# VectorE makes the fourth gate/up unit's low part before the sums of x in four feed-forward layers of a three-layer transformer kernel

## The reference

```python
def swiglu(x, w_gu, w_down):
    gate, up = jnp.split(x @ w_gu, 2, axis=-1)      # w_gu: 1024 x 5632
    return (jax.nn.silu(gate) * up) @ w_down        # w_down: 2816 x 1024

h = h + 0.5 * rmsnorm_2(swiglu(rmsnorm_2(h, g[0]), w_gu, w_down), g[1])
```

## Time and profile before

| what | value |
|---|---|
| time, median of 3 runs | 1271.47 us (1270.14 to 1271.62) |
| profiled execution, from first to last instruction | 1269.6 us |
| TensorE busy (matmul) | 1253.5 us, 99% |
| TensorE weight loads | 1028.9 us, 81% |
| VectorE | 1042.7 us, 82% |
| ScalarE | 804.0 us, 63% |
| GpSimd | 192.4 us, 15% |
| mean DMA rate | 218 GB/s |

### The profile page before, as it was taken

The page is one execution under the profiler, slowest core; times in us unless marked ns, Lnnn a source line. Parts: engine busy times, 40 slices in busy tenths (PEclk is TensorE's granted clock), DMA queues, the critical chain, the costliest instruction groups (busy, mean ns, idle before and its releaser), DMA issues.

```text
span 1269.6 us, 15538 instructions
## 1 busy us (share of the span) xinstructions
PE 1253.5 (99%) x5897; PEld 1028.9 (81%) x5897; DVE 1042.7 (82%) x1035; ACT 804.0 (63%) x986; POOL 192.4 (15%) x224
## 2 busy tenths in 40 slices
PE   9999999999999999999999999999999999999998
PEld 7888878888888878788778888788888877788886
DVE  6766689999799996767899997999977568999984
ACT  6674576665576664645766664766656466766662
POOL 6142130110001100102201101111001003301100
PEclk9999999999999999999999999999999999999999
DMA  9537498997649955568979978389745535999931
GB/s 333 174 100 231 133 313 254 268 270 248 201 151 255 269 168 180 188 226 215 320 249 245 271 251 255 116 237 274 219 166 173 184 125 168 315 286 262 266 135 44
DMA packets 143002, 277.32 MB, mean 218 GB/s; under 512 B 8992, under 2 KB 39896, under 8 KB 142928
## 3 DMA queue, kind: packets, MB, share of 16 engines
q1 hardware_dynamic: 120192, 229.67, 51.6%
q0 software_dynamic: 22288, 45.54, 19.7%
q10 hardware_dynamic: 448, 1.12, 0.2%
HBM read 275.24 MB, written 1.05 MB: 218 GB/s over the span
## 4 chain that ended last, share of the span: by engine, by line
PE 77%; DVE 12%; issue 4%; ACT 3%; DMA 3%; POOL 0%; DVEq 0%; SPq 0%; ACTq 0%
PE B L2102 14%; PE B L2104 14%; PE B L2103 14%; DVE w_lo L1359 7%; PE B L2558 6%; PE B L2560 6%; PE B L2559 6%; PE T L2102 3%; PE T L2104 3%; PE T L2103 3%; DMA VD<-in_ffn_w_gu 2%; DVE VD L1378 1%; DMA Z<-in_ffn_w_gu 1%; ACT w_hi L1082 1%; ACT w_hi L768 1%
## 5 line engine op out<-in xcount | busy, mean ns | idle before, releaser
L1359 DVE TENSOR_TENSOR w_lo<-w_raw,w_hi 128x2048 fp32r<-128x2048 f32 x129 | 296.5, 2299 | 87.5 <-ACT w_hi L768 87.2
L768 ACT ACTIVATE w_hi<-w_raw 128x2048 fp32r<-128x2048 f32 x129 | 247.1, 1918 | 102.7 <-PE B L2560 60.3
L2102 PE MATMUL B<-w_hi,xt_lo 128*128 128x512 f32 x652 | 260.5, 400 | 5.1 <-DVE w_lo L1359 2.1
L2104 PE MATMUL B<-w_hi,xt_hi 128*128 128x512 f32 x652 | 254.7, 391 | 0.0
L2103 PE MATMUL B<-w_lo,xt_hi 128*128 128x512 f32 x652 | 254.0, 390 | 0.0
L2558 PE MATMUL B<-w_hi,act_lo 128*128 128x512 f32 x440 | 172.5, 392 | 0.8 <-DVE w_lo L1359 0.4
L2560 PE MATMUL B<-w_hi,act_hi 128*128 128x512 f32 x440 | 171.4, 390 | 0.0
L2559 PE MATMUL B<-w_lo,act_hi 128*128 128x512 f32 x440 | 171.3, 389 | 0.0
L2102 PEld LDWEIGHTS B<-w_hi,xt_lo 128*128 128x128 f32 x652 | 122.4, 188 | 36.1 <-issue 6.2
L2104 PEld LDWEIGHTS B<-w_hi,xt_hi 128*128 128x128 f32 x652 | 122.4, 188 | 26.4
L2103 PEld LDWEIGHTS B<-w_lo,xt_hi 128*128 128x128 f32 x652 | 122.6, 188 | 23.3
(11 more groups left out here) (330 smaller groups left out, 2110.0 us busy)
## 6 DMA issues: line engine op xcount, KB each, us to landing
w_raw<-in_ffn_w_down SPq DMA_DIRECT2D x88, 512.0 KB, 5.8
Z<-in_ffn_w_gu SPq DMA_DIRECT2D x64, 512.0 KB, 8.1
w_raw<-in_ffn_w_gu SPq DMA_DIRECT2D x48, 512.0 KB, 5.2
nat<-in_ffn_w_gu SPq DMA_DIRECT2D x32, 512.0 KB, 7.8
QT<-in_ffn_w_gu SPq DMA_DIRECT2D x32, 512.0 KB, 7.0
Z<-in_ffn_w_gu POOLq DMA_DIRECT2D x32, 512.0 KB, 8.8
w_raw<-in_conv_w_in SPq DMA_DIRECT2D x24, 512.0 KB, 4.7
w_raw<-in_w_down SPq DMA_DIRECT2D x22, 512.0 KB, 6.6
```

What stands on the lines that cost most here:

```text
L768: act.activation(whi[home(u)][:, :], raw[slot][:, :], ACT.Copy).then_inc(w_hi, 1)
L1359: dve.tensor_tensor(wlo[home(u)][:, :], src, whi[home(u)][:, :].bitcast(F32), ALU.subtract).then_inc(w_lo, 1)
L2102: pe.matmul(bank[:, :], lo[:, k, x], whi[s][:, c], start=first, stop=False, skip_group_check=more)
L2104: return pe.matmul(bank[:, :], hi[:, k, x], whi[s][:, c], start=False, stop=last, skip_group_check=more)
```

## The change

N1b's low part, which VectorE made after the four sums of x in all layers, moves: in layer 1 ahead of x's total and the sums, in layers 3, 4 and 5 between x's total and the sums. In layer 2 it stays where it was (the diff writes it in another way: `split_at(u0 + 3)` and `weights("N1b")` issue the same instruction with the same wait). Nothing is changed on the other engines.

```diff
--- before.py
+++ after.py
@@ -1750,6 +1750,7 @@
             def ffn(f, stat, reader, gain, update=lambda t: None, kv=False):
                 u0 = U_FFN[f]
                 if f == 0:
+                    split_at(u0 + 3)
                     total = x_total(reader)
                 else:
                     update(0)
@@ -1814,8 +1815,11 @@
                     hi, lo = act_parts(d)
                     dve.tensor_tensor(lo[:, :], act_bank(d)[:, :], hi[:, :].bitcast(F32), ALU.subtract).then_inc(act_lo, 1)
 
+                if f >= 2:
+                    split_at(u0 + 3)
                 x_sums(total)
-                weights("N1b")
+                if f == 1:
+                    split_at(u0 + 3)
                 block("P1", 0)
                 dve.wait_ge(rstd, 2 * ST[stat] + 2)
                 act_of(0, PAIR[0] if f else F0)
```

## The result

| kernel | median, us | runs |
|---|---|---|
| before | 1271.25 | 1269.42 to 1271.62 |
| changed | 1276.07 | 1274.0 to 1277.65 |

The ratio is 1.0042, with a 95% interval of 1.0031 to 1.0054: the changed kernel is slower by 4 to 7 us. The forecast was 1275.8 us, range 1272.6 to 1277.8.

A forecast was written before the change was run, and what follows sets the result against it. TensorE was taken as the bound (77% of the span), stopped by VectorE's late work. 2.3 + 2.6 - 0.27 - 0.27 = +4.4 us made span 1274.0; with the 1.9 us margin kept, 1275.8 us, range 1272.6 to 1277.8.

The forecast's parts named there:

- The four stalls at N1b: TensorE's stalls at the fourth gate/up unit, layers 1, 3, 4, 5: real delay 0.97 us, then 0.54 each; all would go.
- two paths to P7: Layer 1's delay at P7: +2.2 us by VectorE's queue with 0.44 slack, +2.3 by TensorE's P2 and ScalarE's P3 high part.
- The claim that layers 1 and 5 pass P7's shift on unbroken: No later wait absorbs it after P7 in layers 1 and 5: what P7 gains or loses, the kernel gains or loses.
- Layers 1 and 5: P7 later by 2.3 and 2.6 us; first activation product later by 2.68 and 3.04 us, after late sums and table load.
- Layers 3 and 4: No table load; first product only 0.1 us late, P2 waits for the second, P7 earlier by 0.25 to 0.3 us each.
- What costs nothing: One down unit's prefetch starts 2.8 to 4 us sooner, without cost; T4, T1 and T2 sums are not moved.
- The room that the range left for the clock: Room above because TensorE's new stalls, up to 1.9 us, exceed the 1.14 us at which clock 1.00 was seen.
- The table page: Skill page adding 1.38 us of draining per ScalarE table switch, 2.8 us more in all; left out of the sum.
- The faster case: Rival: N1b's stalls go, 2.6 us gained, and the late gate is hidden: 1268.9 us; chance 6 in 100.
- that rival's sum: Rival: ScalarE loads its table while waiting for the sums, layers 1 and 5: +1.8 us, 1273.3 us; chance 10 in 100.
- The rival of a dearer gate: Rival: another 1.28 us each in layers 1 and 5, longer switch or slow TensorE restarts: 1278.4 us; chance 8 in 100.
- The last step: From the profiled span, 1269.6 us, to run time: the 1.9 us margin to the median taken as unchanged.

The follow-up runs named there:

- experiment 9: On top of both together, VectorE makes P7's and D0's low parts ahead of weight sum T4, one result ahead of P4's low part: 1299.37 us.
- experiment 8: Both kernels run and profiled once more, unedited: changed kernel 1276.53 us, ratio 1.0038; kernel before 1271.92 us in one run.
- Experiments 3 to 5: Changed kernel with, in turn, early table alone, mended order alone and both together: 1273.12, 1273.3 and 1270.59 us.
- early table alone: Changed kernel plus a one-column Silu on ScalarE before its wait for the sums of x, layers 1 and 5: 1273.12 us, ratio 1.0017.
- mended order alone: Changed kernel with x's total ahead of N1b's low part (layer 1), N1b's high part ahead of the sums of squares (layer 5): 1273.3 us.
- both together: Changed kernel with the early table load and the mended order: 1270.59 us, 1269.85 us in a second set, ratio 0.9989 both times.

## Why the prediction was right

*What bounds the kernel.* The four stalls at N1b went, and P7's stall stayed. The prediction had two paths to P7 and took VectorE's queue as the one that sets it; the traces show the other. P7's first load follows P2's by 11.97 us before (190.71 to 202.68 in the earlier trace rows) and by 11.89 in layers 1, 4 and 5 of the changed kernel, and by 11.87 to 11.98 in every profile but that of experiment 9: P3's high part starts when TensorE has used P2, 3.1 to 3.2 us behind P2's first load, P3's low part 1.95 us later, P7 6.8 us behind that. In the changed kernel's layer 1 VectorE has done P6's low part at 198.40 and starts P3's at 198.53 only, when the high part is there (196.59 + 1.92 = 198.51). So P7 hangs on the second activation product, which lets P2 start, and less on how full VectorE's queue is behind it. The two paths gave +2.2 and +2.3, so the forecast did not depend on the choice.

The claim that layers 1 and 5 pass P7's shift on unbroken holds: from P7 of layer 1 to P7 of layer 2 both kernels take 176.3 us, and from P7 of layer 5 to the end of the span 143.7. For layer 4 it holds in the first profiles, while the second of the changed kernel has a stall of 1.02 us there (experiment 8).

*Layers 1 and 5.* Forecast +2.3 and +2.6, measured +2.34 and +2.67. Every link was where the sum put it: VectorE's waits for N1b's high part 0.94 and 1.44 us (forecast 1 and 1.4), ScalarE's idle time 5.16 and 3.21 (5 and 3.2), the first product 2.77 and 3.13 us late (2.68 and 3.04). TensorE's new waits were under-sized, 1.47 and 2.19 us against 1.3 and 1.9: the row counts from the end of the last weight load, the product was 0.1 us later than forecast, and the loads behind the first wait catch up, so that TensorE stands before P2 sooner than the sum had it. Experiments 3 to 5 split the cause: early table alone leaves +0.9 and +1.25, mended order alone +1.2 and +1.1, both together -0.2 and -0.3. The two parts add, and together they are the whole loss.

*Layers 3 and 4.* Forecast -0.27 each, measured -0.24 and -0.26. The removed stall of 0.54 us did not count in full, since P2 then waits for the second activation product (0.47 us in layer 4's row).

*What costs nothing.* The earlier prefetch shows nowhere in the edited stretches. The room that the range left for the clock was not needed: it is 1.00 in the new waits, and filling them left the stretches as they were.

*The table page.* On the cost of a switch, the Trainium skill ("ScalarE: Activation LUTs", "What ACT_TABLE_LOAD costs") adds about 1.38 us of draining to the load. This case's trace does not agree: the load sits 0.02 us behind one activation and 0.01 us ahead of the next in the changed kernel too, and taking it out of the path gave 1.42 to 1.45 us. The sum without the drain was the right one.

*The rivals.* The faster case needed the product under 0.44 us late; it was 2.8 and 3.1. The compiler did not move the load into the wait by itself; when it was put there by hand the time was 1273.1, where that rival's sum said 1273.3. The rival of a dearer gate (1278.4) needed a longer switch or a slow restart of TensorE: the gate stands 0.01 us behind the load, and the clock stayed 1.00.

*The total.* +4.4 forecast, +4.5 in the edited stretches, +4.8 in the medians. The last step, that all other stalls move along unchanged, holds for the mean only. In single executions of one kernel the time from P7 of layer 2 to P7 of layer 3 wanders by up to 2.5 us (271.6 and 274.1 in the two profiles of the changed kernel), and from P7 of layer 4 to that of layer 5 by 1.1 (296.5 and 297.6). The forecast took one profile's span and the runs' margin over it as a base; that such a profile can lie 2 us off is not in its sum.

## What to carry to other kernels

An operation that waits for nothing may still be the one that others wait for: before moving work ahead of it, follow what it releases on the other engines to where it comes back. Here a stall of 0.5 to 1 us was traded, in layers 1 and 5, for a wait for the unit's own high part and for a round trip over ScalarE (high part of the sums, table load, gate) that had just been covered. A dummy activation of one column, placed in an idle stretch ahead of the wait, takes a table load off the path; and a short stretch between two fixed marks, read in two profiles, tells 0.05 us where the medians tell 1 to 2.

## What the runs showed of the hardware

A table load cost more than its row: 1.28 us in the row, 1.41 us from the start of the sums' high part to the start of the gate (3.23 against 1.82), since the two activations overlap by 0.1 us only without a load between them. And the granted clock stayed at 1.00 through stalls of 1.5 and 2.2 us that end 5.2 us apart, and in the 4 us after them. After the stall of 4.25 us in experiment 9 it was 0.57 over the next 4 us, which mixes the levels of 2.4 and 1.2 GHz, and 1.00 again in the 4 us after that; behind the stalls of 3.8 to 4.1 us in its other four layers it was 0.50 to 0.67.
